# Expert passes that hold 96 rows of one expert of a pair and 32 of the other, instead of 64 and 64

## The reference, cut to what matters

```python
g_logits = hf @ w_group + b_group                       # 4 groups, the best one is taken
e_logits = (hf @ w_erouter[g] + b_erouter[g]) of that group   # 8 experts in a group
top_vals, top_idx = lax.top_k(e_logits, 2)
top_w = softmax(top_vals) * g_w
for e in range(32):
    hid = silu(h @ w_gate[e]) * (h @ w_up[e])           # 1024 -> 256, twice
    y = y + gates[..., e:e + 1] * (hid @ w_down[e])     # 256 -> 1024
```

```
pair   0     1     2     3     4     5     6     7
rows 21,12 46,10 62,28 14,57 17,16 95,17 18,65 45,35
pair   8     9    10    11    12    13    14    15
rows 15,81 27,16 41,18 18,76 16,38  7,18  7,26 41,21
```

## Time and profile before

| | us |
|---|---|
| median of 3 runs | 652.24 |
| the profiled execution, its own time | 651.7 |
| its span, first to last instruction | 649.8 |
| PE busy | 551.8 (85%) |
| DVE busy | 297.3 (46%) |
| ACT busy | 185.7 (29%) |
| POOL busy | 82.2 (13%) |
| first up product of pass 0 starts | 303.73 |
| last down product ends | 567.9 |

### The profile page before, as it was taken

The page is one execution under the profiler, slowest core; times in us unless marked ns, Lnnn a source line. Parts: engine busy times, 40 slices in busy tenths (PEclk is TensorE's granted clock), DMA queues, the critical chain, the costliest instruction groups (busy, mean ns, idle before and its releaser), DMA issues.

```text
span 649.8 us, 7753 instructions
## 1 busy us (share of the span) xinstructions
PE 551.8 (85%) x2628; PEld 322.9 (50%) x2629; DVE 297.3 (46%) x551; ACT 185.7 (29%) x348; POOL 82.2 (13%) x106
## 2 busy tenths in 40 slices
PE   1999999985779898897997889999999998729980
PEld 1788887753456687543332233333333332228870
DVE  3339868998872924474211111211121121175754
ACT  4831411346742432121101010110111010154554
POOL 0650000000000030002112012112211211000000
PEclk9999999996779989989999899999999999958995
DMA  8902102545004001664899998699899999265012
GB/s 342 384 3 72 67 9 58 219 144 211 1 0 195 1 1 66 266 283 168 323 418 419 421 421 348 235 419 385 335 417 422 368 421 419 119 259 210 2 43 86
DMA packets 34248, 145.86 MB, mean 224 GB/s; under 512 B 6576, under 2 KB 6832, under 8 KB 21808
## 3 DMA queue, kind: packets, MB, share of 16 engines
q1 hardware_dynamic: 27168, 133.70, 51.6%
q0 software_dynamic: 6480, 10.50, 4.4%
q10 hardware_dynamic: 576, 1.34, 0.5%
HBM read 142.90 MB, written 14.68 MB: 242 GB/s over the span
## 4 chain that ended last, share of the span: by engine, by line
PE 55%; DVE 19%; DMA 15%; ACT 7%; issue 2%; SPq 1%; POOL 0%; DVEq 0%; ACTq 0%; POOLq 0%
PE bank L1518 17%; DMA wring<-w_up_in 12%; PE bank L1266 10%; PE bank L1534 7%; DVE mix L888 6%; PE bank L1379 6%; PE bank L1563 2%; PE bank L1290 2%; DVE wring L946 2%; PE bank L1360 1%; PE bank L1497 1%; DMA c<-cst_in 1%; PE bank L1347 1%; PE bank L1444 1%; PE bank L1314 1%
## 5 line engine op out<-in xcount | busy, mean ns | idle before, releaser
L1518 PE MATMUL bank<-wring,arena 128*64 128x512 f32 x640 | 142.8, 599 | 13.7 <-SPq L506 12.0
L1518 PEld LDWEIGHTS bank<-wring,arena 128*64 128x64 f32 x640 | 46.2, 138 | 107.4 <-issue 90.1
L888 DVE SCALAR_TENSOR_TENSOR mix<-arena,pr,mix 128x512 f32<-128x512 f32 x120 | 81.5, 751 | 0.0
L1534 PE MATMUL bank<-wring,arena 128*64 128x512 f32 x320 | 73.1, 599 | 9.5 <-ACT arena L800 9.5
L1176 DVE TENSOR_TENSOR arena<-arena,bank 128x256 f32<-128x256 f32 x20 | 8.4, 422 | 148.7 <-ACT arena L797 148.7
L797 ACT ACTIVATE arena<-bank 128x256 f32<-128x256 f32 x20 | 7.7, 384 | 143.9 <-PE bank L1518 143.9
L1534 PEld LDWEIGHTS bank<-wring,arena 128*64 128x64 f32 x320 | 21.2, 136 | 48.5 <-issue 34.3
L1181 DVE COPY arena<-bank 128x512 f32<-128x512 f32 x20 | 13.8, 692 | 66.4 <-PE bank L1534 66.4
L1266 PE MATMUL bank<-hT_hi,win_hi 128*128 128x512 f32 x128 | 33.5, 398 | 1.5 <-DVE hT_lo L866 0.9
L803 ACT ACTIVATE arena<-bank 128x512 f32<-128x512 f32 x20 | 11.9, 597 | 75.8 <-PE bank L1534 75.8
L1266 PE MATMUL bank<-hT_lo,win_hi 128*128 128x512 f32 x128 | 31.6, 389 | 0.0
(11 more groups left out here) (203 smaller groups left out, 812.0 us busy)
## 6 DMA issues: line engine op xcount, KB each, us to landing
wring<-w_gate_in SPq DMA_DIRECT2D x32, 1024.0 KB, 10.4
wring<-w_up_in SPq DMA_DIRECT2D x32, 1024.0 KB, 12.7
wring<-w_down_in SPq DMA_DIRECT2D x32, 1024.0 KB, 15.6
wring<-w_in_in SPq DMA_DIRECT2D x5, 2048.0 KB, 19.1
wring<-w_out_in SPq DMA_DIRECT2D x2, 2048.0 KB, 8.0
wring<-y_d SPq DMA_DIRECT2D x8, 512.0 KB, 6.8
xs<-x_in SPq DMA_DIRECT2D x4, 512.0 KB, 7.5
xs<-x_in SPq DMA_DIRECT2D x1, 2048.0 KB, 8.0
```

What stands on the lines that cost most here:

```text
L888: ins = dve.scalar_tensor_tensor(out=mixc[:, mm, :], in0=u[:, mm, j:j + S], scalar=w, in1=mixc[:, mm, :], op0=ALU.mult, op1=ALU.add)
L1518: ins = pe.matmul(pb[2 + s][a * CAP:(a + 1) * CAP, :], xgT[:, s, k, a * CAP:(a + 1) * CAP], up_w(w, a)[:, :, k, :], start=(k == 0), stop=( ...
L1534: ins = pe.matmul(pb[6 + half][a * CAP:(a + 1) * CAP, :], hidT[:, s, k, a * CAP:(a + 1) * CAP], dn_w(w, a)[:, k, half * 512:(half + 1) * 5 ...
```

## The change

A pass now holds up to 96 rows of one expert (partitions 0 to 95) and up to 32 of the other (partitions 96 to 127). In pairs 2 to 15 the expert with more rows takes the 96; in pairs 0 and 1, whose weights are loaded before the counts are known, it is always the first (`FIXED`). A pair needs as many passes as the worse of (rows of the larger)/96 and (rows of the smaller)/32, rounded up. By the table of rows above that is two passes for pair 7 (45 and 35) and one for each other pair, 17 in all, and the loop of two per turn runs 18. Before, pairs 5, 6, 8 and 11 had an expert with more than 64 rows, which gave 20.

PE issues four products of 32 stationary columns instead of two of 64 for each slice, three of them with the larger expert's weights. Since the weights must stand in the ring in the pair's order, DVE writes a table `order`, and SP reads the expert's number from it before each copy. The routing gets the steps that find the larger expert and keep two scales of rows (counts of the smaller one are multiplied by 3, so that one table of thresholds serves both), and its tables grow from 34 to 50 lists and from 7 to 15 thresholds.

```diff
-CAP = 64
+BIG, SMALL = 96, 32
+PARTS = tuple((lo, lo + SMALL, lo // BIG) for lo in range(0, P, SMALL))
+FIXED = 2
+FAR_ON = 64
-MOST = PAIRS + 2 * S // CAP
+MOST = PAIRS + 2 * S // SMALL
-STEPS = S // CAP - 1
+STEPS = S // SMALL - 1
...
+            def expert(g, a):
+                if isinstance(g, int) and g < FIXED:
+                    return 2 * g + a
+                return number(sp, order[0:1, bass.ds(g, 1), a], 0, NE - 1)
...
-                                 src[bass.ds(2 * g + a, 1)].rearrange("e (p k) n -> p (e k) n", k=DK)
+                                 src[bass.ds(expert(g, a), 1)].rearrange("e (p k) n -> p (e k) n", k=DK)
...
-            chosen_value(SIDE, table8(C_SIDE, NE))
...
-            emptied(dve.tensor_tensor(thr, bk("count")[:, 0:NE].rearrange("p (e j) -> p e j", j=1).broadcast_to([P, NE, STEPS]),
-                                      c[:, C_THR:C_THR + STEPS].rearrange("p (e j) -> p e j", e=1).broadcast_to([P, NE, STEPS]),
-                                      ALU.is_gt), "count")
+            tokens = bk("count")[:, 0:NE].rearrange("p (g a) -> p g a", a=2)
+            step(dve.tensor_copy(beyond[:], bk("count")[:, 0:NE]))
+            pairs = beyond[:].rearrange("p (g a) -> p g a", a=2)
+            step(dve.tensor_tensor(larger[:, FIXED:, 0], pairs[:, FIXED:, 0], pairs[:, FIXED:, 1], ALU.is_ge))
+            step(dve.tensor_scalar(larger[:, FIXED:, 1], larger[:, FIXED:, 0], -1.0, 1.0, ALU.mult, ALU.add))
+            step(dve.tensor_scalar(pairs, larger[:], float(1 - BIG // SMALL), float(BIG // SMALL), ALU.mult, ALU.add))
+            emptied(dve.tensor_tensor(pairs, pairs, tokens, ALU.mult), "count")
+            step(dve.tensor_tensor(thr, beyond[:].rearrange("p (e j) -> p e j", j=1).broadcast_to([P, NE, STEPS]),
+                                   c[:, C_THR:C_THR + STEPS].rearrange("p (e j) -> p e j", e=1).broadcast_to([P, NE, STEPS]),
+                                   ALU.is_gt))
...
-            step(dve.tensor_tensor(H, T0, X, ALU.add))
-            step(dve.scalar_tensor_tensor(out=T1, in0=X, scalar=-float(CAP), in1=R, op0=ALU.mult, op1=ALU.add))
-            step(dve.tensor_tensor(KEY, T1, SIDE, ALU.add))
+            step(dve.tensor_scalar(LOW, T0, float(FAR_ON), None, ALU.is_lt))
+            dve.scalar_tensor_tensor(out=H, in0=LOW, scalar=float(FAR_ON), in1=T0, op0=ALU.mult, op1=ALU.add)
...
+            even = c[0:1, C_IOTA:C_IOTA + NE].rearrange("p (g a) -> p g a", a=2)
+            dve.tensor_tensor(order[:, :, 0], even[:, :, 0], larger[0:1, :, 1], ALU.add)
+            dve.tensor_tensor(order[:, :, 1], even[:, :, 0], larger[0:1, :, 0], ALU.add)
...
                 for k in range(DK):
-                    for a in range(2):
-                        ins = pe.matmul(pb[2 + s][a * CAP:(a + 1) * CAP, :], xgT[:, s, k, a * CAP:(a + 1) * CAP],
-                                        up_w(w, a)[:, :, k, :], start=(k == 0), stop=(k == DK - 1))
+                    for lo, hi, a in PARTS:
+                        ins = pe.matmul(pb[2 + s][lo:hi, :], xgT[:, s, k, lo:hi], up_w(w, a)[:, :, k, :],
+                                        start=(k == 0), stop=(k == DK - 1))
...
                     for k in range(FK):
-                        for a in range(2):
-                            ins = pe.matmul(pb[6 + half][a * CAP:(a + 1) * CAP, :], hidT[:, s, k, a * CAP:(a + 1) * CAP],
+                        for lo, hi, a in PARTS:
+                            ins = pe.matmul(pb[6 + half][lo:hi, :], hidT[:, s, k, lo:hi],
                                             dn_w(w, a)[:, k, half * 512:(half + 1) * 512], start=(k == 0), stop=(k == FK - 1))
```

More of the change, by code:

```diff
@@ L71 @@
 C_RANK = C_SIN + S
-C_SIDE = C_RANK + NE
-C_GRP = C_SIDE + NE
+C_GRP = C_RANK + NE
 C_TOK = C_GRP + NG
@@ L1113, in _ @@
             firsts = scan[:, 2, zero - 1:zero - 1 + PAIRS]
-            step(dve.tensor_copy(beyond[:].rearrange("p (g a) -> p g a", a=2),
-                                 firsts.rearrange("p (g a) -> p g a", a=1).broadcast_to([P, PAIRS, 2])))
+            step(dve.scalar_tensor_tensor(out=pairs, in0=larger[:], scalar=float(FAR_ON),
+                                          in1=firsts.rearrange("p (g a) -> p g a", a=1).broadcast_to([P, PAIRS, 2]),
+                                          op0=ALU.mult, op1=ALU.add))
             banks.wait_full(dve, "rank")
```

39 lines of the change are left out of this document (24 added, 15 removed).

## The result

The changed kernel is slower, and by more than the forecast of 654.4 us and its range (650 to 661) allowed.

What follows compares the result with a forecast made beforehand. It took the expert loop as DMA-bound for one-pass pairs and PE-bound for two-pass pairs. Terms -16.7 + 2.7 + 12.4 + 3.2 + 1.0 + 0 - 0.4 = +2.2 us gave a 654.4 us median, range 650.0 to 661.0.

Steps and rivals of the forecast that it cites:

- The frame: Expert loop: DMA-bound, 18 passes, one hole at pair 7, padding pass behind the last weights; chance 0.74.
- Step 3: Loop's end: the empty eighteenth pass stands wholly on the path behind the last real one, +12.4 us.
- Step 4: Routing ahead of pass 0: added DVE steps and larger tables lengthen it, +3.2 us, bounds 2.7 to 4.0.
- Step 7: After the loop: the last scatter is empty, the last real one hides behind the padding pass, -0.4 us.
- steps 1 and 2: Weight copies in the loop: four DMA holes of two-pass pairs go, -16.7 us; a new one at pair 7, +2.7.
- the low clock: PE after waits near 3.8 us: 1.7 us each in pass 7 or 16, left to the range.
- step 5: SP's expert-number reads before copies: +0.5 us at the loop's first copy, +0.5 in pair 7's hole.
- pair 7's hole closes: Rival, copy queue between pairs 7 and 9: it lasts, 2.7 + 0.5 go, 651.2 us, no change; chance 0.12.
- Step 6: PE's loop products: four tiles run side by side as two do, a pass keeps 12.4 us, +0.
- The rival of slow tiles: PE's product groups take 1.3 times as long, a pass grows by 3.1 us, time 665.8; chance 0.08.
- what would show it: Trace signs: right if pass 0 near 307, one hole, end near 571; wrong if pass 0 after 308, several holes.

Runs made afterwards that it cites:

- experiment 1: Changed kernel with the odd last pass alone behind the loop, 17 passes instead of 18: 652.42 us, ratio 1.0007 to the kernel before.
- Experiment 2: Changed kernel with one pass for every pair, 16 in all, three rows of pair 7 multiplied with other weights: 651.41 us, ratio 0.998.
- experiment 3: Kernel before with each product of 64 stationary columns issued as two of 32, still 20 passes: 654.92 us, ratio 1.003.
- experiment 10: Changed kernel with the two code copies of multiply for odd passes in swapped order: 662.23 us, ratio 1.0154 to the kernel before.
- experiment 5: Changed kernel run once more, unchanged: 663.71 us, ratio 1.0191 to the kernel before.
- experiment 6: Changed kernel with one more embedding product moved ahead of PE's wait for the list: 661.43 us, ratio 1.014 to the kernel before.
- experiment 7: Changed kernel with SP reading a pair's two expert numbers once, ahead of its wait for up_done: 662.55 us, ratio 1.0168.
- experiment 8: Changed kernel with odd last pass alone, one embedding product ahead of the list wait, and SP's reads ahead of its wait: 651.34 us, ratio 1.0006.
- experiment 4: Changed kernel with its table, reads and four tiles, but the 64/64 split of before, 20 passes: 666.63 us, ratio 1.0232.
- experiment 11: Changed kernel with odd last pass alone, SP's reads ahead of its wait and swapped code copies: 645.92 us, ratio 0.9879 to the kernel before.
- experiment 9: Kernel before with products split into four tiles, plus swapped order of the odd passes' two code copies: 656.06 us, ratio 1.0042.
- experiment 12: Changed kernel with three tiles, 64 and 32 columns for the larger expert, 32 for the smaller: 858.17 us, ratio 1.3125.

## Why the prediction was wrong, point by point

- **The frame held.** 18 passes with 1152 recorded products, a DMA at 420 GB/s with one hole about pair 7, the padding pass wholly behind the last weights: all as described. Step 3 (+12.4) measured +12.5, and experiment 1 takes 12.8 us of the median away. Step 4 (routing +3.2) measured +3.05. Step 7 fits (-0.3).
- **Where the gap lies.** Of the 10.3 us between the sum (+2.2) and the measured +12.5, 4.1 lie in the stretch of the copies (steps 1 and 2), 3.0 in the low clock ahead of the first copy, 2.5 upstream of the change and 0.6 in step 5.
- **Steps 1 and 2 failed in size: -14.0 forecast (-13.5 with the 0.5 of step 5 that falls into the same stretch), -9.4 measured.** I took four stretches under 420 GB/s out of the sum as if the rest of the loop would keep its rate without them. The middle did: 420 GB/s from 348.76 to 430.76 and 419 from 442.76 to 548.76. When the holes went, the DMA lost time elsewhere: 0.9 us more in the early windows, 2.0 in the last 6.8 us, where before it had stood at 408, and 3.5 instead of 2.7 in pair 7's hole. The 16.2 us of a pair is right for its bytes at 420 GB/s, but the whole segment comes to 16.8 a pair. Experiment 2 has no hole at all, and its segment is no shorter. The rival "pair 7's hole closes" asked the right question and overpriced the answer: closing it won nothing that shows within the 2 us by which segments of the same loop differ.
- **Step 6 failed: "four tiles, 0".** The products do overlap fully (experiment 3). What I had not counted is the code. By the order of instructions each copy of `multiply` had twice as many products, and I asked only whether PE could issue them in time, not where it gets them. Experiment 3 puts the price at 3.5 us of segment and 1.003 [1.0002, 1.0058] of the time. In after it adds 2.5 us ahead of pass 1 and most of 3.8 ahead of pass 3; how much of that reaches the end is not separated, and swapping the copies gave no clear gain in the time (experiment 10).
- **The low clock** had no term in the sum. It was named and left to the range, but for passes 7 and 16. It came elsewhere: on the list product and on pass 0, 0.6 + 1.7 us, and probably on what stands between them (+0.7), 3.0 in all ahead of the first copy, where nothing hides it. Pass 0's up products took 8.64 us or more in the profiled runs of experiments 2, 5, 6, 7, 8 and 10 and of after, and 7.07 in those of 1, 4 and 11; in before and in experiments 3 and 9, with the short routing, never. Step 4's upper bound of 4.0 held this to 0.8.
- **Step 5** was +1.1 at the first copy instead of +0.5: the read costs some 0.7 us (copies 1.14 apart instead of 0.46), twice in front of the first two transfers. Experiment 7 takes it away and shows no clear gain.
- **2.5 us of the profiled run lie upstream of the change and are scatter.** The profiled runs with the routing of after start `lg` anywhere from 275.90 (experiment 1) to 281.19 (experiment 12), those with the routing of before from 276.85 to 278.17. After's own run has a clock of 0.63 in the window from 190 to 204 us (first row) against 0.88 before (second) and 0.88 in experiment 5, the same kernel:

```profile
190.00:204.00 14.00, 10.52 (x67) 8.80 (x68) 8.35 (x16) 7.10 (x17) 1.54 (x2) 0.63 0.08 11
```
```profile
190.00:204.00 14.00, 10.36 (x77) 7.94 (x78) 8.23 (x16) 8.01 (x17) 2.72 (x2) 0.88 0.22 78
```

  The per-run clocks (0.913 to 0.924) say that after keeps a lower mean clock than before (0.945), part of which is the loop's own waits (0.94 against 0.99 in the segment). A fixed upstream part of a microsecond or so is not excluded.
- **The rival of slow tiles** gave 665.8 and the median is 665.19. It is a right number for a wrong reason: its 3.1 us a pass are nowhere, since every full-clock pass took 7.05 to 7.08.
- **By "what would show it"** two signs fired as wrong: pass 0 later than 308 (310.60), and dips in the rate beside the one hole. The loop's end came at 580.7 instead of near 571.

What stays open: whether the loading of code is all of PE's "issue" idle time (a packet of the instruction queue stands at the front of each stretch and the swap moves it, but no packet's use is recorded); why some DMA engines run out of work before others as the last weights come; what holds the clock low in front of pass 0, since experiment 6 brought an idle stretch of its own; experiment 4's high runs.

## What to carry to other kernels

When a loop is rounded up to whole turns, ask where the padding turn stands: behind the last load it costs its full length, however idle its engine was before. Removing holes in the copies won 9.4 us here of the 14.0 that their lengths promised, so compare the mean rate of the whole stretch with the peak, start and end too, before booking a hole. And when a change multiplies instructions inside branches, the code is a cost of its own in the first turns. Keep tiles of one width, and look whether the first turn falls through or jumps.

## What the runs showed of the hardware that was not expected

- Four column tiles of 32 ran as fast as two of 64: 7.07 us for 64 recorded products against 7.04 for 32. Three tiles of 64, 32 and 32 columns took 15.95 for 48, with a turn of 1.0 us for each change of width.
- PE idled 2.5 to 4.9 us ahead of passes 1 and 3 once its loop body had twice the products, in every profiled execution with four tiles in the order of after (after and experiments 1 to 8); exchanging two copies of the code took the first of these away. Each such stretch has a packet of the instruction queue inside it or less than 1 us ahead; once the loop's code had come, jumps inside the loop cost no more packets (none from 372 us to its end).
- The same kernel's time follows the granted clock from run to run: 647.0 at 0.928 and 654.5 at 0.914 (experiment 1).
